# Constant matmuls issued on TensorE during its stops, in a two-layer kernel with mixture of experts, sparse attention and retrieved experts

## What is computed

```python
# block 1
n = rms_norm(h, g_mix);  z = n @ w_in + b_in
m = sigmoid(ga) * (chunked_attention(q, k, v) @ w_pa) + sigmoid(gc) * (short_conv(u, bg, cg) @ w_pc)
h = h + m @ w_o                                    # residual "wo"
h = h + hier_moe(rms_norm(h, g_ffn))               # 32 experts, 2 for each token
gate = sigmoid(rms_norm(h, g_ple) @ w_ple_gate + b_ple_gate)
h = h + gate * (p @ w_ple_proj)
# block 2
z = rms_norm(h, norm_mix_2) @ w_in_2               # norm "mix2"
h = h + concat(gla_mixer(...), nsa_mixer(...)) @ w_out_2   # residual "wout"
h = h + cross_attn(rms_norm(h, norm_xattn_2), ...)         # norm "xa", residual "xo"
h = h + peer_ffn(rms_norm(h, norm_ffn_2), ...)     # norm "peer"
return rms_norm(h, norm_final_2)
```

## Time and profile before

| | |
|---|---|
| three runs | 1956.68, 1957.86, 1959.43 us; median 1957.86 us |
| the profiled execution | 1958.08 us, with a span of 1956.4 us from first to last instruction |
| busy, share of the span | TensorE 1704.1 us (87%), VectorE 896.4 us (46%), ScalarE 718.9 us (37%) |
| mean granted clock | 0.92 |
| TensorE instructions | 10537 matmul rows and as many weight loads |
| DMA | 418.15 MB, 214 GB/s over the span |

### The profile page before, as it was taken

How to read it: one execution, slowest core, us unless ns; L and a number is a source line. 1 busy time by engine, 2 the same in 40 slices (tenths; PEclk the granted TensorE clock), 3 DMA queues, 4 the chain that set the end, 5 groups by cost and what they waited for, 6 DMA issues and landing times. The chain is left out here.

```text
span 1956.4 us, 25891 instructions
## 1 busy us (share of the span) xinstructions
PE 1704.1 (87%) x10537; PEld 1329.9 (68%) x10537; DVE 896.4 (46%) x1528; ACT 718.9 (37%) x1436; POOL 5.6 (0%) x25
## 2 busy tenths in 40 slices
PE   7999877666665677898897899989999999999997
PEld 6988543223332233588557599989999988888886
DVE  3563320000000001236534249998788876666665
ACT  3452121101001001343333344444677755555554
POOL 1000000000000000000000000000000000000000
PEclk9999888888888887897598999999999999999999
DMA  9434459999999996433001115544443446556653
GB/s 343 170 132 144 172 240 422 421 421 421 421 421 422 421 421 254 172 130 108 1 25 62 65 40 186 185 162 163 161 134 134 133 148 194 194 192 194 194 194 133
DMA packets 84946, 418.15 MB, mean 214 GB/s; under 512 B 14091, under 2 KB 16592, under 8 KB 51930
## 3 DMA queue, kind: packets, MB, share of 16 engines
q1 hardware_dynamic: 73440, 398.59, 54.3%
q10 hardware_dynamic: 11386, 17.87, 2.7%
HBM read 415.36 MB, written 1.06 MB: 213 GB/s over the span
## 5 line engine op out<-in xcount | busy, mean ns | idle before, releaser
L2420 DVE TENSOR_TENSOR tab_lo<-arena,tab_hi 128x1024 fp32r<-128x1024 f32 x256 | 312.5, 1225 | 122.9 <-ACT tab_hi L1869 120.7
L1048 PE MATMUL bank<-arena 128*32 128x512 f32 x1536 | 226.8, 743 | 147.6 <-DMA arena<-in_w_dram 146.1
L1869 ACT CAST tab_hi<-arena 128x1024 fp32r<-128x1024 f32 x256 | 267.9, 1047 | 0.2
L1048 PEld LDWEIGHTS bank<-arena 128*32 128x32 f32 x1536 | 63.0, 132 | 284.4 <-issue 282.4
L1453 PE MATMUL bank<-x_hi,tab_lo 128*128 128x256 f32 x1024 | 145.0, 285 | 7.9 <-DVE tab_lo L2420 7.9
L1453 PE MATMUL bank<-x_hi,tab_hi 128*128 128x256 f32 x1024 | 148.3, 288 | 2.0 <-ACT tab_hi L1869 2.0
L1453 PE MATMUL bank<-nT_lo,tab_hi 128*128 128x256 f32 x1024 | 143.0, 281 | 0.0
L2102 DVE TENSOR_TENSOR arena<-arena,bank 128x512 f32<-128x512 f32 x8 | 5.5, 688 | 294.3 <-PE bank L1066 294.3
L1486 PE MATMUL bank<-tab_hi,e_hi 128*128 128x512 f32 x512 | 137.7, 391 | 1.8 <-DVE arena L2459 1.8
L1453 PEld LDWEIGHTS bank<-x_hi,tab_lo 128*128 128x128 f32 x1024 | 132.5, 193 | 8.3 <-DVE tab_lo L2420 8.3
L1486 PE MATMUL bank<-tab_hi,e_lo 128*128 128x512 f32 x512 | 137.7, 391 | 0.0
(11 more groups left out here) (393 smaller groups left out, 2297.9 us busy)
## 6 DMA issues: line engine op xcount, KB each, us to landing
arena<-in_w_dram SPq DMA_DIRECT2D x192, 1024.0 KB, 21.0
arena<-in_peer_down_dram SPq DMA_DIRECT2D x128, 512.0 KB, 3.5
arena<-in_peer_up_dram SPq DMA_DIRECT2D x128, 512.0 KB, 3.5
arena<-in_packed_first_dram SPq DMA_DIRECT2D x28, 1024.0 KB, 7.2
arena<-in_packed_later_dram SPq DMA_DIRECT2D x28, 1024.0 KB, 7.1
arena<-in_mem_w_dram ACTq DMA_DIRECT2D x8, 1024.0 KB, 10.0
arena<-in_packed_later_dram SPq DMA_DIRECT2D x2, 816.0 KB, 14.3
arena<-in_packed_later_dram SPq DMA_DIRECT2D x2, 768.0 KB, 19.8
```

The lines of the kernel that those rows point to most:

```text
L1048: mm = nc.tensor.matmul(dst[SLOTS * e:SLOTS * e + SLOTS, :], lhsT=lhsT, rhs=moe_weights(step, e)[:, k, :], start=k == 0 and step in (0, 2, ...
L1869: nc.scalar.copy(tab_hi[n % HI][:, :], tab[n % PR]).then_inc(S("table_hi"), 1)
L2420: nc.vector.tensor_tensor(tab_lo[n % PR][:, :], tab[n % PR], tab_hi[n % HI][:, :].bitcast(F32), ALU.subtract).then_inc(S("table_lo"), 1)
```

## The change

A new function `hold_clock(pe, out, n)` issues n matmuls of `ident` by `ones` (128 x 128 x 128, float32) into a piece of a PSUM bank that nobody reads at that time. It waits for nothing and signals nothing. It is called:

- in `residual_pe` before the second `norm_turn`, 11 matmuls, so three times in the kernel;
- after residual "wo", 6; after the router's products, 16; after the count of rows and ahead of the barrier, 9;
- at the end of the expert branch and ahead of the barrier, 16; after the transposes of `p`, 6;
- between the two turns of norm "mix2", 14, and after them, 6;
- in each of the 16 units of sparse attention, after `nsa_scores`, 2;
- after residual "wout", 10.

That is 148 matmuls. No other instruction is added, removed or moved.

```diff
+        def hold_clock(pe, out, n):
+
+            for _ in range(n):
+                nc.tensor.matmul(out, lhsT=ident[:, :], rhs=ones[:, :], start=True, stop=True)
+
         def residual_pe(pe, tag, at, src, norm):
...
+            hold_clock(pe, bank[0][:, P:2 * P], 11)
             norm_turn(pe, norm, 1)
...
             residual_pe(pe, "wo", 12, mT, "ffn")
+            hold_clock(pe, bank[5][:, 0:P], 6)
             wait_nT(pe, "ffn", KT)
...
                 project_tok(pe, ("router", t), wgr, KT, 0, 36, t, nT, br36[0:1, :])
 
+            hold_clock(pe, bank[1][:, 0:P], 16)
             pe.wait_ge(S("picked_ready"), 1)
...
                              stop=True).then_inc(S("rows_counted"), 1)
+            hold_clock(pe, bank[1][:, 0:P], 9)
             phase_end(pe, "pe")
...
                     scatter(BATCHES - 1, half)
+                hold_clock(pe, bank[0][:, 0:P], 16)
...
             mm.then_inc(S("p_turned"), 1)
+            hold_clock(pe, bank[0][:, 0:P], 6)
             pe.wait_ge(S("pT_ready"), 1)
...
-            norm_pe(pe, "mix2")
+            norm_turn(pe, "mix2", 0)
+            hold_clock(pe, bank[0][:, P:2 * P], 14)
+            norm_turn(pe, "mix2", 1)
+            hold_clock(pe, bank[4][:, 0:P], 6)
             wait_nT(pe, "mix2", KT)
...
                     nsa_scores(i)
+                    hold_clock(pe, bank[6][:, 0:P], 2)
...
             residual_pe(pe, "wout", LATE_AT + 9, catT, "xa")
+            hold_clock(pe, bank[5][:, 0:P], 10)
```

## The result

Six runs of the changed kernel gave 1941.77 to 1947.21 us, median 1943.31 us; six of the kernel before beside them gave 1956.68 to 1959.43 us, median 1957.95 us. The ratio is 0.993, with a 95% interval of 0.9918 to 0.9941: 14.6 us faster, where 6.5 us were forecast. 1943.3 us is inside the stated range of 1942 to 1960 us, outside the forecast's own 1948 to 1954 us, and at the time given for rival B.

The account below looks back on a forecast made before the run. Expert matmuls wait for weights by DMA; in sparse attention TensorE is the bound, at half clock. The terms -2.8 - 2.9 - 2.7 - 1.2 - 0.5 + 3.6 = -6.5 us take 1957.9 to 1951.4 us; range 1942 to 1960 us.

Parts of the forecast that it names:

- the forecast's own 1948 to 1954 us: Whole kernel: the prediction's main case around 1951.4 us, given a chance of 0.42.
- rival B: Sparse attention turns fast early, -4.5 us there; -14.6 us in all, 1943 us; chance 0.22, all faster.
- The stops with nothing behind them but the chain: Residual "wo" to first expert: 0.35 turn, 1.15 count, 1.65 gathering, less 0.3 at the barrier: experts 2.8 us earlier.
- a faster turn: Eight transposes at 1.04 instead of 1.97 us; 0.35 us comes through at each of four turns, 1.4 us.
- I take 0: End of expert branch: the 16 matmuls don't delay TensorE's leaving, because the sequencer, not the array, leaves; cost 0 us.
- the bound of 1.2 us: End of expert branch: TensorE's lateness if it begins to leave only after its matmuls are through.
- -2.9: Behind the experts: transposes save 0.5 us and L717 2.4 us at full clock; from 2.9 down to -0.7 saved.
- I take a rise at unit 10: Sparse attention: clock rises at unit 10; the holds' price less the halved time before the old rise gives +3.6 us.
- this fifth: Sparse attention: units with holds resemble, in all but a fifth of their time, those running 41 us without a rise.
- The price of the holds: Sparse attention: two holds cost 0.86 us at half clock, making a unit 3.89 us, or 0.46 us at full.
- See only a shift: Peer layers from 1157 us on: no gain or loss of their own, only moved in time.

## Why the prediction was right in sign and short in size

The mechanism that was forecast is the one at work: full-size matmuls in the stops keep or bring back the clock, and the branch and the attention are where the sum was most uncertain. In both of these the value chosen was wrong, and the point forecast of 1951.4 us missed the 1943.3 us for that reason.

**The stops with nothing behind them but the chain: right.** From the second turn to the first expert the forecast was 2.8 us and the rows give 0.5 + 0.7 + 1.6 = 2.8 us, term by term. That holds where the clock stays up behind the 16, as in seven of eleven profiles of this code; in the other four it fell again in the count and 1.1 us came, so the agreement is in part luck. "mix2" gave 2.5 us for 2.7, "wout" and "xo" 2.0 for 1.7. The turns took 1.09 us at each place; the Trainium skill ("TensorE: Matmul & The Clock Gate", Part 4: PE-mode transpose), by which full clock doesn't engage for transposes, is not borne out here for the pace of float32 transposes, neither by the earlier trace rows nor by these; whether transposes by themselves would keep the clock, no run here tells. What came through of a faster turn was 0.25 us at "wo", "mix2" and "wout", for 0.35, and nothing at "xo" (2.28 us from the turn to the next transposes in both). At "xo" 1.1 us came for 0.5 because the first products of L835 ran at full clock though no hold stands behind the turn.

**"I take 0" for leaving the branch: wrong.** It cost 2.7 us, and even the bound of 1.2 us was too low. The prediction put this stop on VectorE's path, 2.6 us from its last addition to the restart, and the earlier trace rows had it otherwise: the 5.17 us ended with TensorE's own sequencer (PEq L460). TensorE's way out takes 4.15 to 4.3 us behind its last holding matmul, as 16 and 32 show, and 5.1 to 5.2 us behind the last scatter where there are none, in the kernel before too; only some 0.9 us of matmuls fit in. The reason given, that the sequencer leaves and not the array, didn't help: the instruction packet comes only behind the matmuls. Whether the sequencer waits for the array or is held up while it issues the matmuls, no run separates. Behind that, L717 gave 1.8 us for 2.4, the transposes and the copy behind them 0.3 for 0.5, and the gate's fall took back 1.4 us, which no term had. So -2.9 became +2.0 us, a miss of 4.9 us.

**"I take a rise at unit 10": wrong, and the largest term.** The rise came at unit 4, and +3.6 us became -6.4, a miss of 10 us; it is rival B's mechanism, whose time of 1943 us is the measured one, though B had -4.5 us for it. The argument was that the units with holds resemble, in all but a fifth of their time, those that ran 41 us without a rise. The runs show that this fifth decides: in all ten profiles with full-size holds in the attention the rise came between unit 3 and unit 8, in the three without at unit 12, and with 8-column holds at unit 14. A measure of resemblance by time was the wrong one. The price of the holds was about right: two slow units of one block took 7.97 us in the kernel without the 16 (945.94 to 953.91 us), 3.99 us each, against a forecast 3.89 us, and a hold of two took 0.55 us at full clock against 0.46 us. Timeline of the changed kernel, scores of units 3, 4 and 8:

```profile
948.40 1.22 PE L1364 MATMUL bank<-arena 64*128 64x256 f32 x2
...
952.60 0.83 PE L1364 MATMUL bank<-arena 64*128 64x256 f32 x2
...
961.46 1.12 PE L1364 MATMUL bank<-arena 64*128 64x512 f32 x2
```

The four units from 4 to 8 took 8.86 us, the same before 12.11 us (955.79 to 967.90 us). But where the rise comes at unit 8, as in two profiles, the attention takes 57.3 us and the holds gain nothing; at unit 6, as with 32 in the branch, it takes 53.3 us. The point from which they pay lies between the two.

**"See only a shift": wrong.** `peer_ffn` gave 3.6 us in these two profiles. The same code took 802.8 to 802.9 us in three profiles, 806.3 us in that of the kernel before, and 808.1 to 808.3 us in six in which the clock fell in its scores.

**Why 14.6 us and not 6.5.** The misses are -10.0 us in the attention, +4.9 behind the experts, -3.6 in `peer_ffn`, and -1.4 us ahead of the first hold and in the experts; that makes -10.1 us and, with the -6.5, 16.6 us of the span, against 16.4. The medians are 1.8 us nearer to each other than the spans. Two wrong steps thus had opposite signs. That the measured time is rival B's 1943 us is therefore partly luck: its mechanism, the early rise, came true, but its sum had -4.5 us for the attention, where -6.4 us came, -2.9 us behind the experts, where +2.0 us came, and nothing for `peer_ffn`, the experts and the start, where -5.0 us came.

**What stays open.** Where in the attention the clock rises isn't set by the code alone. The kernel without the 16, with and without holds in the scores, is the same program up to the end of the attention, and its two profiles have the rise at unit 4 and at unit 8; that is 7.6 us (49.67 against 57.30 us). Why one or the other comes, and why the clock falls in the scores of one run and not of another behind the same stop, no run settled. The changed kernel had the good outcome of both in its two profiles, and its eleven runs in two groups lie within 1941.8 to 1947.2 us, all with a mean granted clock of 0.937 to 0.940; the two at 1947 us had 0.938 and 0.939, so the mean clock doesn't explain them. That the branch's 16 bring this about, by where they place the rest in time, is an argument and not shown. No experiment moved the attention in time without changing something else. Nor were the stops taken out one by one: apart from the branch, the share of each rests on its rows in a few profiles.

## What to carry to other kernels

Holding matmuls pay in stops that another engine sets and that they fit into, and with 128 columns; narrow ones of 8 columns cost as much of the engine and slowed this kernel by 1.0%, and no width between was run. Don't put them where the engine then has something of its own to do before it can go on, as leaving a branch, beyond the few that fit: 16 cost 2.7 us at that place and 3 next to nothing, though the kernel without the 16 was no faster as a whole. Ask of a stop first which engine ends it: here the row said so, PEq, before anything was changed. Inside a stretch without gaps (64-row scores, attention) they are paid in full and return only what an earlier rise gives; measure there by several runs, for a run here differed from another of the same kernel by up to 13 us.

## What was not expected of the hardware

TensorE's restart behind the taken branch came 2.83 to 2.86 us after the start of one packet of instructions in every profile, and 4.15 to 4.32 us after the last of 16 or 32 holding matmuls. Matmuls put ahead of it delay it nearly one for one once they no longer fit: 16 more, 3.6 us of them, delayed it by 3.4 us.

Matmuls of 64 rows took longer where a matmul of 128 rows stood between every eight of them, without any change of the clock: eight rows in 1.09 us instead of 0.80 us, at a granted clock of 1.00.

A float32 matmul of 8 columns occupied TensorE 0.22 us a row at half clock, against 0.21 us for one of 128 columns in the earlier trace rows.

One kernel can have two times: the kernel without the branch's 16 ran in 1941 us twice (granted clock 0.938 and 0.941) and in 1952 to 1953.5 us nine times (0.926 to 0.930), on one chip.
